# A transformer kernel's last projection as seven block products with tokens as rows, and its residual turned to rows early

## What is computed

```python
a   = (a * silu(za)) @ w_att_out
sgo = (sgo * silu(zs)) @ w_sg_out
y   = ga * a + gs * sgo            # gates, both 512 x 1024
x   = x + y @ w_o                  # w_o 1024 x 1024: the last projection
out = x * rsqrt(mean(x * x, axis=-1) + 1e-6) * final_g
```

## Time and profile before

| | before |
|---|---|
| median of the runs | 1296.03 us |
| the profiled execution's own time | 1295.99 us |
| span of its profile | 1294.2 us |
| PE, PEld busy | 99%, 86% |
| DVE, ACT, POOL busy | 63%, 48%, 54% |
| TensorE clock granted, mean | 0.999 of full |

### The profile page before, as it was taken

The page is one execution under the profiler, slowest core; times in us unless marked ns, Lnnn a source line. Parts: engine busy times, 40 slices in busy tenths (PEclk is TensorE's granted clock), DMA queues, the critical chain, the costliest instruction groups (busy, mean ns, idle before and its releaser), DMA issues.

```text
span 1294.2 us, 20065 instructions
## 1 busy us (share of the span) xinstructions
PE 1287.6 (99%) x7784; PEld 1116.6 (86%) x7784; DVE 818.7 (63%) x1253; ACT 622.6 (48%) x1004; POOL 703.7 (54%) x504
## 2 busy tenths in 40 slices
PE   9999999999999999999999999999999999999998
PEld 8877777887888889989988998877778899999887
DVE  3674544555544599448834867656646999996434
ACT  6223534556532565325522546445557556665233
POOL 4463343425444578648865866443333876666551
...
GB/s 207 94 119 105 42 155 42 155 41 94 99 85 86 82 101 122 89 109 98 99 110 87 113 91 170 106 70 70 103 66 65 98 99 98 99 98 98 102 93 66
DMA packets 143626, 127.10 MB, mean 98 GB/s; under 512 B 4464, under 2 KB 138736, under 8 KB 143536
## 3 DMA queue, kind: packets, MB, share of 16 engines
...
...
...
## 4 chain that ended last, share of the span: by engine, by line
PE 99%; DMA 1%; ACT 0%; DVE 0%; issue 0%; SPq 0%; ACTq 0%
PE gemm L813 17%; PE gemm L814 17%; PE gemm L821 16%; PE gemm L1125 9%; PE gemm L1130 9%; PE gemm L1126 9%; PE gemm L870 2%; PE gemm L871 2%; PE gemm L876 2%; PE gemm L837 2%; PE gemm L838 2%; PE gemm L843 2%; PE mix L1251 1%; PE mix L1239 1%; PE mix L1228 1%; DMA xtm<-x 1%
## 5 line engine op out<-in xcount | busy, mean ns | idle before, releaser
L678 POOL TENSOR_TENSOR wlo<-raw,whi 128x512 fp32r<-128x512 f32 x280 | 388.2, 1419 | 307.3 <-ACT whi L1415 287.8
L813 PE MATMUL gemm<-hh,whi 128*128 128x512 f32 x584 | 232.1, 397 | 0.0
L814 PE MATMUL gemm<-hl,whi 128*128 128x512 f32 x584 | 227.8, 390 | 0.0
L706 POOL TENSOR_TENSOR wlo<-raw,whi 128x512 fp32r<-128x512 f32 x108 | 159.5, 1503 | 47.0 <-ACT whi L1624 41.6
L1415 ACT ACTIVATE whi<-raw 128x2048 fp32r<-128x2048 f32 x66 | 126.1, 1910 | 45.2 <-PE gemm L821 26.1
L821 PE MATMUL gemm<-hh,wlo 128*128 128x512 f32 x584 | 145.9, 390 | 0.0
L813 PEld LDWEIGHTS gemm<-hh,whi 128*128 128x128 f32 x584 | 109.7, 188 | 26.7 <-issue 4.0
L814 PEld LDWEIGHTS gemm<-hl,whi 128*128 128x128 f32 x584 | 109.8, 188 | 22.0 <-issue 0.2
L821 PEld LDWEIGHTS gemm<-hh,wlo 128*128 128x128 f32 x584 | 109.2, 188 | 22.4
L1125 PE MATMUL gemm<-hh,whi 128*128 128x256 f32 x496 | 124.7, 284 | 0.0
L1126 PE MATMUL gemm<-hl,whi 128*128 128x256 f32 x496 | 124.3, 283 | 0.0
...
## 6 DMA issues: line engine op xcount, KB each, us to landing
raw<-w_in SPq DMA_DIRECT2D x53, 1024.0 KB, 5.3
...
raw<-w_o SPq DMA_DIRECT2D x8, 1024.0 KB, 5.0
...
raw<-w_ao SPq DMA_DIRECT2D x4, 1024.0 KB, 4.9
raw<-w_so SPq DMA_DIRECT2D x4, 1024.0 KB, 5.0
...
```

Of the source, the lines that this page charges most:

```text
L678: last = nc.gpsimd.tensor_tensor(a(wlo), a(raw), as_f32(a(whi)), ALU.subtract)
L706: return nc.gpsimd.tensor_tensor(part_of(wlo, u, b), raw_block(u, f, k), as_f32(part_of(whi, u, b)), sub)
L813: mm(bank[:, :], w, xh[:, k, :], start=(k == 0), stop=False)
L814: mm(bank[:, :], w, xl[:, k, :], start=False, stop=False)
```

## The change

The last projection y @ w_o is cut into 2 x 2 blocks: left and right 256 tokens, k-tiles 0 to 3 and 4 to 7, features 0 to 511 and 512 to 1023. Seven products of 256 tokens x 512 k x 512 features stand for eight, in the order P1, P5, P2, P6, P7, P3, P4. Tokens are now the stationary side and 512 weight columns move; a product is two banks (128 tokens each) of 12 matmuls, and results come out as token rows. Their operands are blocks and sums of blocks:
- of y2 (token side): four sums, `u_sum[:, 0]` after tile 3, the other three in `late_sums` as tiles 5, 6 and 7 arrive; ACT splits them, DVE takes the rests (`late_rests`).
- of w_o: P1, P2, P4 use plain blocks (`wa[0]`, `wb[0]`, `wb[1]`), P7 a difference that POOL makes, P5, P6, P3 sums that DVE makes in `w_sum` in SBUF, one after the other. ACT splits all seven (`block_high`); POOL takes the rests of P1, P2, P7 and P4, DVE those of P5, P6 and P3.

Two of w_o's four megabyte blocks are loaded into buffers of their own ahead of w_so, and the final gain comes as a row spread over the partitions. The residual `xT` is turned to rows during the w_so units (`turn_input`, one turn behind each tile, two behind tile 6) and ACT keeps it in `xr`. DVE and POOL combine the seven results with it; the mean square is one ACT Square with a sum along the row for each half (a 128 x 512 piece), and the root is taken from both. The gain is multiplied in at the end. Copies in rows, row sums on PE and the half-width last unit go.

The diff, cut to its core:

```diff
...
+        wa = [place(f"wa{f}", [P, 4, 512], Z0 + 32 + 8 * f) for f in range(2)]
+        w_sum = place("w_sum", [P, 4, 512], Z0 + 72)
+        w_hi = [place(f"w_hi{i}", [P, 4, 512], Z0 + 16 * i, f32r) for i in range(2)]
+        w_lo = [place(f"w_lo{i}", [P, 4, 512], Z0 + 16 * i + 8, f32r) for i in range(2)]
+        xr = [place(f"xr{t}", [P, DM], Z0 + at) for t, at in enumerate((80, 96, 100, 64))]
+        fg2b = place("fg2b", [P, DM], Z0 + 68)
+        sq_junk = place("sq_junk", [P, 512], Z0 + 104)
...
+        W_SLOT = [(wide(whi, n_o2 % 2), wide(wlo, n_o2 % 2)), (wide(whi, (n_o2 + 1) % 2), wide(wlo, (n_o2 + 1) % 2)),
+                  (w_hi[0], w_lo[0]), (w_hi[1], w_lo[1])]
+        L_P1, L_P5, L_P2, L_P6, L_P7, L_P3, L_P4 = range(7)
+        LAST_SLOT = (0, 1, 2, 3, 0, 1, 2)
+        B1, B2 = M[0:2], M[2:4]
+        B3, B4 = [[bank_of(T_END + 2 * i + t) for t in range(2)] for i in range(2)]
+        TURNS = ((2, 0), (2, 1), (0, 0), (0, 1), (1, 0), (1, 1), (3, 0), (3, 1))
...
+        K_GROUPS = (slice(0, 2), slice(2, 3), slice(3, 4))
...
+            sp.wait_ge(sem("mixed_ps"), KD)
+            for f in range(2):
+                sp.dma_start(wa[f][:, :, :], cols(w_o2, f * 512, 512, 0, 4)).then_inc(sem("wT_in"), 16)
             stream(n_gs + 4, 4, both(tiles_of(w_so, 0)))
-            stream(n_o2, 4, both(tiles_of(w_o2, 0)))
...
+            for i, f in enumerate((1, 0)):
+                slot_free(n_o2 + i)
+                load(n_o2 + i, cols(w_o2, f * 512, 512, 4, 4), wb[f])
+            sp.wait_ge(sem("y2_sum"), KD)
+            sp.dma_start(fg2b[:, :], fg2_row.partition_broadcast(P)).then_inc(sem("c2_in"), 16)
...
+            def block_rest(i, block):
+                high, low = W_SLOT[LAST_SLOT[i]]
+                pool.wait_ge(sem("hi_done"), N_UNITS + i + 1)
+                for k in range(4):
+                    last = nc.gpsimd.tensor_tensor(low[:, k, :], block[:, k, :], as_f32(high[:, k, :]), sub)
+                last.then_inc(sem("lo_done"), 1)
+            block_rest(L_P1, wa[0])
+            block_rest(L_P2, wb[0])
+            pool.wait_ge(sem("s_made"), 3 * N_SEVEN + 1)
+            for k in range(4):
+                last = nc.gpsimd.tensor_tensor(wa[1][:, k, :], wa[0][:, k, :], wa[1][:, k, :], sub)
+            last.then_inc(sem("s3_made"), 1)
+            pool.wait_ge(sem("o_copied"), 8)
+            for t in range(2):
+                pool.wait_ge(sem("p1_read"), N_SEVEN + 1 + t)
+                o = xr[t][:, 0:512]
+                nc.gpsimd.tensor_tensor(o, o, p1_s(t), ALU.add).then_inc(sem("row_pre"), 1)
+            block_rest(L_P7, wa[1])
+            for t in range(2):
+                pool.wait_ge(sem("p1_read"), N_SEVEN + 3 + t)
+                o = xr[2 + t][:, 0:512]
+                nc.gpsimd.tensor_tensor(o, o, p5_s(t), ALU.add).then_inc(sem("row_pre"), 1)
+                pool.wait_ge(sem("row_pre"), 3 + 2 * t)
+                nc.gpsimd.tensor_tensor(p5_s(t), p5_s(t), xr[2 + t][:, 512:], ALU.add).then_inc(sem("row_pre"), 1)
+            block_rest(L_P4, wb[1])
+            pool.wait_ge(sem("c2_in"), 80)
+            for t, h, count in ((2, 1, 3), (3, 1, 4), (1, 0, 2)):
+                pool.wait_ge(sem("row_sq"), count)
+                o = xr[t][:, h * 512:(h + 1) * 512]
+                nc.gpsimd.tensor_tensor(o, o, fg2b[:, h * 512:(h + 1) * 512], mult).then_inc(sem("row_pre"), 1)
...
+            def turn_input(i):
+                t, h = TURNS[i]
+                if i == 0:
+                    pe.wait_ge(sem("mixed"), KD)
+                if i >= 4:
+                    pe.wait_ge(sem("o_copied"), i - 3)
+                for c in range(4):
+                    last = nc.tensor.transpose(M[i % 4][:, c * P:(c + 1) * P], xT[:, 4 * h + c, t * P:(t + 1) * P], ident)
                 last.then_inc(sem("o_ps"), 1)
+            def turns_after(p, j):
+                if p < 3:
+                    turn_input(2 * p + j)
+                elif j == 0:
+                    turn_input(6)
+                    turn_input(7)
+            for p in range(4):
+                unit_fm(n_gs + 4 + p, sgh, sgl, after=lambda j: turns_after(p, j))
+            def last_product(i, banks, xh, xl, low):
+                high, rest = W_SLOT[LAST_SLOT[i]]
+                pe.wait_ge(sem("hi_done"), N_UNITS + i + 1)
                 for t in range(2):
+                    tok = slice(t * P, (t + 1) * P)
+                    for k in range(4):
+                        mm(banks[t][:, :], xh[:, k, tok], high[:, k, :], start=(k == 0), stop=False)
+                        mm(banks[t][:, :], xl[:, k, tok], high[:, k, :], start=False, stop=False)
+                    if t == 0:
+                        pe.wait_ge(sem(low[0]), low[1])
+                    for k in range(4):
+                        last = mm(banks[t][:, :], xh[:, k, tok], rest[:, k, :], start=False, stop=(k == 3))
+                    last.then_inc(sem("last_ps"), 1)
+            LOW, SUM_LOW = 2 * N_UNITS, 3 * N_SEVEN
+            left, right = slice(0, HALF), slice(HALF, SEQ)
+            pe.wait_ge(sem("o_copied"), 8)
+            pe.wait_ge(sem("y2_lo"), 4)
+            last_product(L_P1, B1, hh[:, 0:4, left], hl[:, 0:4, left], ("lo_done", LOW + 1))
+            pe.wait_ge(sem("t_lo"), 12)
+            last_product(L_P5, B2, u_hi[:, 0], u_lo[:, 0], ("s_lo", SUM_LOW + 1))
+            pe.wait_ge(sem("y2_lo"), KD)
+            last_product(L_P2, B3, hh[:, 4:8, left], hl[:, 4:8, left], ("lo_done", LOW + 2))
+            pe.wait_ge(sem("t_lo"), 21)
+            pe.wait_ge(sem("tile_free"), T_END)
+            last_product(L_P6, B4, u_hi[:, 1], u_lo[:, 1], ("s_lo", SUM_LOW + 2))
+            pe.wait_ge(sem("p1_read"), N_SEVEN + 2)
+            last_product(L_P7, B1, u_hi[:, 2], u_lo[:, 2], ("lo_done", LOW + 3))
+            pe.wait_ge(sem("p1_read"), N_SEVEN + 4)
+            last_product(L_P3, B2, hh[:, 4:8, right], hl[:, 4:8, right], ("s_lo", SUM_LOW + 3))
+            pe.wait_ge(sem("c_sum"), C_END + 2)
+            last_product(L_P4, B3, hh[:, 0:4, right], hl[:, 0:4, right], ("lo_done", LOW + 4))
...
             split(n_gs + 5)
+            keep_input(0)
+            keep_input(1)
+            y2_high(0)
+            y2_high(1)
             split(n_gs + 6)
+            keep_input(2)
+            y2_high(2)
+            keep_input(3)
             split(n_gs + 7)
+            y2_high(3)
+            act.wait_ge(sem("t_made"), 7)
+            fn(u_hi[:, 0], u_sum[:, 0], ACT.Copy).then_inc(sem("t_hi"), 1)
+            keep_input(4)
+            y2_high(4)
+            keep_input(5)
+            act.wait_ge(sem("wT_in"), 48)
+            act.wait_ge(sem("tile_done"), T_END - 2)
+            block_high(L_P1, wa[0])
+            y2_high(5)
+            sum_highs(0)
+            keep_input(6)
+            keep_input(7)
+            y2_high(6)
+            sum_highs(1)
+            act.wait_ge(sem("s_made"), 3 * N_SEVEN + 1)
+            act.wait_ge(sem("tile_done"), T_END)
+            block_high(L_P5, w_sum)
+            y2_high(7)
+            act.wait_ge(sem(f"raw_in{(n_o2 + 1) % 2}"), raw_count(n_o2 + 1))
+            block_high(L_P2, wb[0])
+            keep_product(1, 1, p1_s, B1, 0)
+            sum_highs(2)
+            keep_product(2, 1, p1_s, B1, 1)
+            act.wait_ge(sem("s_made"), 3 * N_SEVEN + 2)
+            block_high(L_P6, w_sum)
+            act.wait_ge(sem("t_lo"), 21)
+            keep_product(3, 3, p5_s, B2, 0)
+            keep_product(4, 3, p5_s, B2, 1)
+            act.wait_ge(sem("s3_made"), N_SEVEN + 1)
+            act.wait_ge(sem("last_ps"), 2)
+            block_high(L_P7, wa[1])
+            square_row(0, 0, 1)
+            square_row(1, 0, 2)
+            act.wait_ge(sem("s_made"), 3 * N_SEVEN + 3)
+            act.wait_ge(sem("last_ps"), 4)
+            block_high(L_P3, w_sum)
+            act.wait_ge(sem("last_ps"), 6)
+            block_high(L_P4, wb[1])
+            square_row(2, 1, 7)
+            square_row(3, 1, 8)
+            square_row(2, 0, 9)
+            row_root(2, 0)
+            square_row(3, 0, 10)
+            row_root(3, 0)
+            row_out(2, 1, 2, 7)
+            square_row(0, 1, 11)
+            row_root(0, 1)
+            row_out(3, 1, 3, 8)
+            square_row(1, 1, 12)
+            row_root(1, 1)
+            row_out(1, 0, 5, 9)
...
+            def late_sums(g):
+                ks = K_GROUPS[g]
+                dve.wait_ge(sem("y2_sum"), 4 + ks.stop)
+                link(tt(u_sum[:, 2, ks], y2[:, later(ks), HALF:], y2[:, ks, HALF:], ALU.subtract))
+                link(tt(u_sum[:, 1, ks], u_sum[:, 2, ks], y2[:, ks, 0:HALF], ALU.add))
+                tt(y2[:, ks, HALF:], y2[:, later(ks), 0:HALF], u_sum[:, 1, ks], ALU.subtract).then_inc(sem("t_made"), 1)
+            def late_rests(g):
+                ks = K_GROUPS[g]
+                dve.wait_ge(sem("t_hi"), 15 + 3 * g)
+                for i in (1, 2):
```

(134 more changed lines are left out.)

202 lines of the change are left out of this document (33 added, 169 removed).

## The result

After the change the kernel takes **1310.4 us** (median of 4 runs, 1310.23 to 1311.25) against 1296.01 of the kernel before (4 runs): ratio **1.0112**, 95% interval 1.0095 to 1.013. It is slower by 1.1%, and slower was the forecast; the 1312 us was 1.6 us too high. The profiled execution took 1310.34, 1.7 more than its span.

A forecast was written before the change was run, and what follows sets the result against it. PE was taken to bound the kernel, full to the end. Terms -6.2 + 18.7 + 3.7 = +16.2 us on the span of 1294.2 gave 1310.4, so a run of 1312 us; range 1299 to 1321.

The forecast's parts named there:

- Term 1: PE's own work from w_so to the end: 85.5 us instead of 91.8, so -6.2 us.
- Loads at nothing: Two 1 MB loads ahead of w_so's first, w_o's other two megabytes and the final gain arrive in time: no cost.
- Term 2: PE stalls in the last projection, waiting for operands DVE, ACT and POOL prepare: +18.7 us, the longest 6.3 before P7's low half.
- the list: Each engine's instructions from 1195.4 laid out by hand in program order with measured prices, giving the predicted waits and times.
- The cause, turns at SBUF: DVE and POOL instructions on two SBUF tensors take turns, one each; nothing overlaps but POOL's last 0.16 us.
- the +4 of the bound: Upper bound on turn-taking: DVE gives way twice in a 2048-column block, adding 4 us in all.
- DVE behind from tile 4 on: Token and block sums and rests delay DVE around tile 4; tile 6 is read at 1245.2, tile 7 at 1251.6.
- Term 3: Tail from PE's end to the last scaling: 7.2 us instead of 3.5, since DVE is behind again, so +3.7 us.
- Rival 1: DVE and POOL do not hinder each other in the last projection, preparation hides, run takes 1291 us; 13%.
- Rival 2: Clock falls to half in the stall before P7's low half, 40 matmuls cost 9 us more; net +3 to +8, 1315 to 1320; 18%.
- Rivals 3 and 4: Last-projection stalls of only 6 to 13 us, 1299 to 1307, 14%; saving and stalls cancel within 0.2%, 5%.

The follow-up runs named there:

- experiment 6: Against the changed kernel, last stage rewritten with less SBUF work: 1300.5 us; its order alone then changed: 1290.5; order and DVE/POOL side changed: 1289.4 us.
- experiment 5: Changed kernel plus 22 matmuls that nobody reads before P7's low half, where PE waits for POOL's rest: 1310.44 us.
- experiments 1 to 4: Changed kernel with POOL's last-stage work cut: 1291.3 us; DVE's block instructions cut: 1300.8; POOL's instructions merged or halved: 1312.35, 1311.3; POOL's blocks given to DVE: 1305.0.
- experiment 3: Changed kernel with POOL's block rests and block difference in one instruction instead of four: 1312.35 us; in eight: 1311.3 us.

## Why the prediction was right

- **Term 1, -6.2 us.** Right. Without waits PE takes 85.4 us (experiment 6), forecast 85.5, against 91.8 before.
- **Loads at nothing.** Right: no PE wait is released by a DMA, and the tiles end at 1242.9 as forecast.
- **Term 2, +18.7.** Right in place and cause, 2.8 too large. PE ends at 1298.76 (1297.85 and four times 0.227), 103.2 after its start at 1195.6; less 85.5 of work and 1.8 of clock that is 15.9. The idle times in brackets sum to 13.8; each leaves out some 0.3 us, since it counts from the modelled end of the matmul before and the matmuls behind a wait start a little slower. With those 0.3, P7's part was forecast 6.3 and is 6.0, P5's 2.5 and 2.4, P6's 2.9 and 2.8, P1's 1.4 and 1.8, P2's 1.1 and 0.6. Most of the 2.8 is P4's 1.7, which is not there: POOL's rest came at 1294.7, earlier than the 1296.0 of the list, and PE, 1.8 us slowed by the clock, wanted it at 1295.1. At full clock PE would have waited 1.4 (1.34 in experiment 5). So the clock, which the sum had at nothing, stands in the place of that stall, and the two together cost about what the stall alone was forecast to cost: that part of the nearness is no luck, since POOL sets the time there.
- **The cause, turns at SBUF.** Shown by experiments 1 to 4. The step from the one pair of rows of before to "one instruction each, nothing overlaps" held: after the change a block costs DVE at most 3.37 beside POOL, the 2.29 and 1.1 of the list, and never a second turn (the +4 of the bound). The Trainium skill (SBUF — State Buffer, SBUF: two separate sides) says the same, that the pair is held "for the whole instruction". The 4.82 us of experiment 3 agree but for a little: the addition, 0.42 us alone, ended 0.3 us behind the POOL instruction that kept it out, so about 0.1 us overlapped. That the turns alternate held after the change, but not in every kernel (below).
- **DVE behind from tile 4 on.** Tile 6 was read at 1245.24 and tile 7 at 1251.41 (forecast 1245.2 and 1251.6).
- **Term 3, +3.7.** The way is as forecast (DVE's additions at 1288.8 to 1295.3 beside POOL, then the last half behind two outputs), 0.5 shorter: 6.7 us from PE's end to 1305.46. The transfers behind took 3.1, not 3.5.
- **Rival 1** (the preparation hides) was wrong for this kernel. It can be made to hide: with less of it at SBUF and in another order the kernel takes 1289.4, near the rival's 1291. The argument for it, that both engines are half idle before, was true of the sum and said nothing of when.
- **Rival 2** (the clock) came, but cost 1.8 us where I had 9 before the next stall's share. The step that failed was that P7's rest and the whole of P3, 40 matmuls, would run at 1.2 GHz; it was nine, 3.9 us of work, and the next stall took the 1.8 us back (experiment 5). The Trainium skill (TensorE: Matmul & The Clock Gate, What's actually happening) has an idle array fall to half clock and need sustained work to come back. Both happened: the clock was 0.50 behind P7's wait and 1.00 again after the nine.
- **Rivals 3 and 4** (stalls of 6 to 13 us; nothing to measure) did not come: the stalls are 15.9 us.

In sum: -6.2 + 15.9 + 1.8 of clock + 3.2 of tail, 0.2 from a later start and 0.4 less behind it: 14.5 by these terms, 14.4 measured on the span (1308.6 less 1294.2).
